# The value half of the compression two slots behind its key half, and its weights asked for behind chunk 10

## The reference

```
h = rms_norm(x)
proj = h @ w_in                  # state-space input, NSA q/k/v, gates, stick-breaking q/k/v
o_ssm = s5_mixer(...)            # diagonal complex state space
o_nsa = nsa_mixer(...)           # compressed + selected + window attention
o_sb  = stick_breaking(...)
x += (sum of gate * (branch @ w_branch)) @ w_out
x += conv_ffn(rms_norm(x))       # up, width-3 causal conv, silu * value, down
```

```
blocks = t[:, idx] + pos
hid = gelu(einsum('bnlhd,lde->bnhe', blocks, w1))    # w1: 32 x 64 x 128 floats, 1 MB
return einsum('bnhe,ed->bnhd', hid, w2)
```

## Time and profile before

| | us |
|---|---|
| median of 3 runs | 954.81 (954.48 to 955.27) |
| the profiled execution, its own time | 954.62 |
| its span | 952.9 |
| TensorE busy | 925.4 |
| VectorE busy | 709.8 |
| ScalarE busy | 592.1 |
| GpSimd busy | 287.9 |

### The profile page before, as it was taken

How to read it: one execution, slowest core, us unless ns; L and a number is a source line. 1 busy time by engine, 2 the same in 40 slices (tenths; PEclk the granted TensorE clock), 3 DMA queues, 4 the chain that set the end, 5 groups by cost and what they waited for, 6 DMA issues and landing times. The chain is left out here.

```text
span 952.9 us, 16037 instructions
## 1 busy us (share of the span) xinstructions
PE 925.4 (97%) x5855; PEld 777.3 (82%) x5855; DVE 709.8 (74%) x1131; ACT 592.1 (62%) x955; POOL 287.9 (30%) x226
## 2 busy tenths in 40 slices
PE   8889999999999999999999999999999999999996
PEld 6789877777878888888889887777787788888885
DVE  6998967666667887888875777766567677777876
ACT  7436776768455665666674567677664566666664
POOL 0523334351420568467100413443315001010110
PEclk9999999999999999999999999999999999999999
DMA  8964434453454756556449744433645456556551
GB/s 235 266 192 141 140 126 133 130 147 132 167 176 138 204 189 207 177 180 212 142 126 299 204 141 133 133 124 99 181 129 177 133 177 212 186 178 213 181 177 44
DMA packets 139559, 159.09 MB, mean 167 GB/s; under 512 B 17153, under 2 KB 106089, under 8 KB 139498
## 3 DMA queue, kind: packets, MB, share of 16 engines
q1 hardware_dynamic: 137960, 156.44, 53.2%
q10 hardware_dynamic: 1538, 1.84, 0.7%
HBM read 154.33 MB, written 1.05 MB: 163 GB/s over the span
## 5 line engine op out<-in xcount | busy, mean ns | idle before, releaser
L1719 DVE TENSOR_TENSOR wl<-ring,wh 128x1024 fp32r<-128x1024 f32 (+1 forms) x276 | 361.1, 1311 | 94.6 <-ACT wh L1384 93.5
L1384 ACT ACTIVATE wh<-ring 128x1024 fp32r<-128x1024 f32 (+1 forms) x276 | 288.2, 1045 | 148.0 <-PE pj L791 114.8
L791 PE MATMUL pj<-h,wh 128*128 128x256 f32 (+1 forms) x1376 | 296.8, 339 | 12.1 <-DVE wl L1719 11.1
L791 PEld LDWEIGHTS pj<-h,wh 128*128 128x128 f32 x1376 | 230.5, 191 | 39.5 <-issue 10.5
L791 PE MATMUL pj<-wh,h 128*128 128x512 f32 (+1 forms) x832 | 259.4, 394 | 3.0 <-DVE wl L1719 1.4
L791 PE MATMUL pj<-h,wl 128*128 128x256 f32 x1024 | 188.9, 283 | 0.0
L791 PEld LDWEIGHTS pj<-wh,h 128*128 128x128 f32 x832 | 148.4, 188 | 41.8 <-issue 8.2
L791 PEld LDWEIGHTS pj<-h,wl 128*128 128x128 f32 x1024 | 157.6, 191 | 6.6
L791 PE MATMUL pj<-wl,h 128*128 128x512 f32 (+1 forms) x416 | 159.7, 384 | 0.0
L2396 POOL TENSOR_TENSOR work<-work 128x512 f32<-128x512 f32 x20 | 41.1, 2055 | 261.7 <-DVE work L2182 198.5
L791 PEld LDWEIGHTS pj<-wl,h 128*128 128x128 f32 x416 | 78.1, 188 | 16.3
(11 more groups left out here) (303 smaller groups left out, 1230.8 us busy)
## 6 DMA issues: line engine op xcount, KB each, us to landing
ring<-in_ffn_w_up SPq DMA_DIRECT2D x44, 1024.0 KB, 5.1
ring<-in_w_in SPq DMA_DIRECT2D x40, 1024.0 KB, 5.1
ring<-in_ffn_w_down SPq DMA_DIRECT2D x22, 1024.0 KB, 4.9
ring<-in_w_in SPq DMA_DIRECT2D x16, 512.0 KB, 5.3
ring<-in_w_branch SPq DMA_DIRECT2D x8, 1024.0 KB, 5.6
ring<-in_w_out SPq DMA_DIRECT2D x8, 1024.0 KB, 5.1
ring<-in_w_branch SPq DMA_DIRECT2D x8, 512.0 KB, 5.9
ring<-in_w_in SPq DMA_DIRECT2D x8, 256.0 KB, 3.9
```

The source lines that it names most:

```text
L791: return nc.tensor.matmul(o, a, b, start=start, stop=stop, skip_group_check=True)
L1384: A(dst, src, ACT.Copy).then_inc(w_hi.sem, 1)
L1719: TT(dst, src, hi.bitcast(F32), ALU.subtract).then_inc(w_lo.sem, 1)
```

## The change

The table of slots gives the two halves slots of their own: hidden 0 and 2, output 2 and 4, with each sum one slot behind its hidden part. The functions of TensorE and ScalarE are cut accordingly, and the copies of `kc` and `vc` are put at the two output slots. SP asks for the value's weights behind chunk 10.

```diff
-CMP_HID, CMP_OUT, CMP_S, CMP_T = 0, 2, 3, 6
+CMP_HID, CMP_OUT, CMP_S, CMP_T = (0, 2), (2, 4), 3, 6
...
# SP
-                    if i == 6:
+                    if i == 10:
                         sp.wait_ge(h_turned.sem, h_turned.at(l, 4))
                         sp.sem_inc(passed.sem, 1)
                         load_cmp(l, 1)
...
# TensorE: cmp_out() loops no longer over r, but takes it
-                def cmp_out():
+                def cmp_out(r):
...
-                    if q == CMP_HID:
-                        for r in range(2):
-                            cmp_hidden(r)
-                    if q == CMP_HID + 1:
-                        for r in range(2):
-                            cmp_sum(r)
-                    if q == CMP_OUT:
-                        cmp_out()
+                    if q in CMP_HID:
+                        cmp_hidden(CMP_HID.index(q))
+                    if q - 1 in CMP_HID:
+                        cmp_sum(CMP_HID.index(q - 1))
+                    if q in CMP_OUT:
+                        cmp_out(CMP_OUT.index(q))
...
# ScalarE
-                    if q == CMP_HID:
-                        for r in range(2):
-                            a.wait_ge(hq_done.sem, hq_done.at(l, r + 1))
-                            A(hp[:, r, :], (bA, bB)[r][:, 0:P], ACT.Copy).then_inc(hq_out.sem, hq_out.up())
+                    if q in CMP_HID:
+                        r = CMP_HID.index(q)
+                        a.wait_ge(hq_done.sem, hq_done.at(l, r + 1))
+                        A(hp[:, r, :], (bA, bB)[r][:, 0:P], ACT.Copy).then_inc(hq_out.sem, hq_out.up())
...
-                    if q == CMP_OUT:
+                    if q == CMP_OUT[0]:
                         a.wait_ge(kc_done.sem, kc_done.at(l, 1))
                         A(kc[:, 0:NC], bO[:, 0:NC], ACT.Copy).then_inc(kc_ready.sem, kc_ready.up())
+                    if q == CMP_OUT[1]:
                         a.wait_ge(kc_done.sem, kc_done.at(l, 2))
                         for r in range(0, P, 32):
                             ins = A(vc[r:r + NC, r // 32, :], bB[r:r + NC, 64:64 + HD], ACT.Copy)
```

More of the change, by code:

```diff
@@ L1005, in cmp_sum @@
                         .then_inc(hid_done.sem, hid_done.up())
-                def cmp_out():
-                    for r in range(2):
[L1010 to L1020, removed]
+                def cmp_out(r):
+                    pe.wait_ge(hid_ready.sem, hid_ready.at(l, r + 1))
+                    for s in range(2):
+                        hs = hid[:, r, NC * s:NC * s + NC]
+                        if r == 0:
+                            ins = mm(bO[HD * s:HD * s + HD, 0:NC], w2[:, 0, :], hs, True, True)
+                        else:
+                            for t in range(NT):
+                                row = 32 * (2 * s + t)
+                                ins = nc.tensor.matmul(bB[row:row + NC, 64:64 + HD], hs, w2[:, 1, :], start=True,
+                                                       stop=True, skip_group_check=True, tile_position=(0, row))
+                    ins.then_inc(kc_done.sem, kc_done.up())
                 def cmp_scores():
@@ L1580, in _ @@
                         branch_hi(slice(2 * n, 2 * n + 2), oS[:, 2 * n:2 * n + 2, :])
-                    if q == CMP_HID:
-                        for r in range(2):
-                            a.wait_ge(hq_done.sem, hq_done.at(l, r + 1))
-                            A(hp[:, r, :], (bA, bB)[r][:, 0:P], ACT.Copy).then_inc(hq_out.sem, hq_out.up())
[L1585 to L1590, removed]
-                    if q == CMP_OUT:
+                    if q in CMP_HID:
+                        r = CMP_HID.index(q)
+                        a.wait_ge(hq_done.sem, hq_done.at(l, r + 1))
+                        A(hp[:, r, :], (bA, bB)[r][:, 0:P], ACT.Copy).then_inc(hq_out.sem, hq_out.up())
+                    if q - 1 in CMP_HID:
+                        r = CMP_HID.index(q - 1)
+                        a.wait_ge(hid_done.sem, hid_done.at(l, r + 1))
+                        A(hid[:, r, 0:2 * NC].rearrange("p (g n) -> p g n", g=2),
+                          (bA, bB)[r][:, P:P + 32].rearrange("p (g n) -> p g n", g=2)[:, :, 0:NC], ACT.Gelu_apprx_tanh)\
+                            .then_inc(hid_ready.sem, hid_ready.up())
+                    if q == CMP_OUT[0]:
                         a.wait_ge(kc_done.sem, kc_done.at(l, 1))
                         A(kc[:, 0:NC], bO[:, 0:NC], ACT.Copy).then_inc(kc_ready.sem, kc_ready.up())
+                    if q == CMP_OUT[1]:
                         a.wait_ge(kc_done.sem, kc_done.at(l, 2))
```

## The result

The changed kernel takes 957.97 us (median of 6 runs, 957.40 to 959.59) against 955.00 of the kernel before (6 runs, 954.48 to 955.93): a ratio of 1.0034 [1.0023, 1.0044], slower by 3.0 us. The forecast was 955.7, and the range ended at 957.4. The profiled execution took 958.56 us with a span of 956.8, against 954.62 and 952.9: 3.9 us more of span, which the two traces let us divide.

The account below looks back on a forecast made before the run. The kernel was taken as a TensorE stream with short holes. First layer 0 plus second layer's slot 6 +0.98, net of the load's 0.71 gain, gave +1.0 us: forecast 955.7, range 953.3 to 957.4.

Parts of the forecast that it names:

- The step that failed: First layer, piece 14: GpSimd's rotation product may slip ahead, TensorE starting 1.0 us later; taken as 0.
- The bound: First layer, piece 14: the slip of GpSimd's product was bounded by -0.5 and +0.4 us.
- sign of being wrong: Wrong if second layer's slot 6 hole is missing, TensorE waits again by slot 8, or pre-slot-0 holes change over 1 us.
- the stretch at 1.2 GHz: First layer: short slow stretch after TensorE's waits; VectorE sets the pace there, so it costs nothing.
- Slot 6 of the second layer: Value copies delay the exponential, VectorE's split and TensorE: slot 6 +0.98 us, with a new 1.6 us hole.
- The load's gain of 0.71 us: Second layer, before slot 0: chunk 7 comes sooner, VectorE's part of piece 15 starts 0.71 us earlier; bounds 0 and 1.5.
- The first layer's slot 6: Exponential could start at 92.20, against 92.18 before; the 0.61 us hole stays: 0, bounds -0.6 and +0.4.
- The value load: Behind chunk 10 its issues fit SP's queue; TensorE needs the weights over 15 us later: no wait, 0.
- A: Rival, slot 4: table load ahead of the copies, exponential and slot 6 1.28 us earlier; sum -0.3, 954.5; 15%.
- C: Rival, second layer: ScalarE's lateness of 3.94 us lasts, TensorE waits again at slot 8, paying 3.0: 957.8; 14%.
- D: Rival, both layers: the exponential doesn't follow its table load at once, standing 0.65 us behind: 957.0; 4%.
- B: Rival, faster: transfers were the root of more than one TensorE hole in both layers: 952.5; 12%.

Follow-up runs that it names:

- e2: Kernel before with only the value-weight load moved behind chunk 10, slots unchanged: 956.67 us, ratio 1.0011 to the kernel before.
- e5: Changed kernel with 20 unused matmuls on TensorE ahead of the first layer's piece 14: 957.54 us, ratio 1.0016 to the kernel before.
- e8: The changed kernel itself timed again, as control of a later group on one chip: 957.23 us, ratio 1.0020 to the kernel before.
- e4: Changed kernel with slot 4's exponential ahead of the value copies, softmax's small operands in their own tile: 955.90 us, ratio 1.0006 to the kernel before.
- e9: Changed kernel with the exponential ahead of the value copies and the load behind chunk 6 in both layers: 955.21 us, ratio 0.9998.
- e1: Changed kernel with the value-weight load back at its old place behind chunk 6: 956.74 us, ratio 1.0018 to the kernel before.
- e10: Changed kernel, exponential first, load moved only in the second layer, idle matmuls before the first layer's pieces 10, 11 and 14: 954.09 us, ratio 0.9989.

## Why the prediction was wrong

- **The step that failed** is the first layer's: "If such a product slips ahead of piece 14, TensorE starts the piece 1.0 us later and has 0.69 us in its next hole to get it back [...] Bounds -0.5 and +0.4, I take 0." The slip happened (e2: 57.13 in place of 59.78), and the start was late by 1.1 us, as bounded. The price was not: 1.64 us in this execution, and by time 1.5 (medians) or 1.1 (ratio) in e2, even with the second layer's gain in it. The prediction's own sign of being wrong, a hole before slot 0 that changes by over 1 us, is the 1.49 that became 2.58. The prediction had dismissed the stretch at 1.2 GHz as costing nothing. That was right for where it lay, over pieces that end in a hole; over piece 14, with TensorE itself behind, it costs 1.45 us. e5 and e8 have the slip without that clock, and lose 0.07 and 0.13 in their profiles. That this part is the clock's is shown by profiles alone; by time e5 gained nothing that could be seen.
- **The bound** was made from the hole alone, as if a longer wait had no other consequence. The trace of the kernel before had the pattern: the slow stretch that the prediction dismissed came behind two holes of 2.00 and 2.05 us (before 41.71 and 46.87) with 3.1 us of work between them. With a term of 0 to +1.6 the range would have held the result.
- **Slot 6 of the second layer** was right in mechanism and size. Without the gain ahead of it the working gives 0.98 + 0.71 = 1.69 for the stretch from the hidden matmuls; it measured 1.77. The hole was put at 1.6 and is 1.41, because TensorE's own stream grew by 0.3 us and not by the 0.1 allowed for the moved matmuls. e4, which changes only this order in the changed kernel, takes it away, and so does e9 against e1.
- **The load's gain of 0.71 us** is there in part. The wait for chunk 7 is gone, and the splits of pieces 14 and 15 stand back to back (528.94) as worked out. But ScalarE's four issues at 518.09 took 3.00 us where the profile before had 2.49, which put the next piece 0.5 us late. It isn't the load's doing: e1, with the load at its old place, shows 3.51, and the profile before was a favourable one. Kernels with the old load need 50.59 (before) and 50.90 us (e1, e9) for the stretch, those with the moved one 50.35 to 50.72 in eight profiles and 49.84 in e10, where the four issues took 2.44 us as in the profile before. Against that one like case the gain is 0.75; where both had slower issues it is 0.2 to 0.55.
- **The first layer's slot 6** came as worked out: exponential at 94.61, 22.9 us behind the hidden matmuls where it was 22.8, and the hole 0.47 in place of 0.61.
- **The value load** is in nobody's way at its new place. It landed in 7.0 us (median), and in the second layer its matmuls came 15.3 us behind the issue (531.86 and 547.19). Right.
- **Rivals.** A is refuted: the load stands behind the copies (557.91). C is refuted: after slot 6 nothing is lost (394.3 against 394.4). D is refuted: load and exponential follow the copies at 0.01 and 0.02 us. The Trainium skill's page "ScalarE: Activation LUTs" ("What ACT_TABLE_LOAD costs") has a drain of some 1380 ns besides; these rows leave no room for one. (Two such drains are an estimated 2.8 us by the page's figure, not the 2.7 of the prediction.) B, that transfers were the root of more than one hole, is refuted: the rows did come sooner, and TensorE's hole before piece 14 grew by 1.1 us, since VectorE, which the earlier trace rows shows full, sets the pace there.

What stays open: what decides in which execution the earlier slow stretch lies over piece 10 or 11, and with it whether the next can meet piece 14, and how often each happens. The starts of the profiles differ by up to 1.8 us at piece 7, but no run fixed that start. Open too is why GpSimd's product and VectorE's operation slow each other; the runs show only the price.

## What to carry to other kernels

Where the pacing engine is full and is slowed by what another engine runs beside it, an earlier transfer can be a loss: ask beside which operation the other engine's work will now run, and whether that operation stands ahead of the one that the critical engine waits for. A hole in TensorE's stream can cost twice, by its length and by the clock behind it, and in these profiles a slow stretch was free only where a hole followed; give such a term its own bound. And in an in-order queue put the copy that nobody waits for behind the operation that heads a chain, table load included: here that order is worth 1.9 us (e9 against e1), and with the first layer's load left where it was the change becomes a gain of 1.1.

## What the runs showed that had not been expected

- A single 128x512 product of GpSimd costs what VectorE does beside it 1.0 to 1.1 us in every place read, whatever that is (eight small operations, one large, a pair of splits), and GpSimd's own takes 1.3 to 2.4.
- Two executions of the same instructions differ in where TensorE is at 1.2 GHz, and one placement costs 1.5 us more than the other (18.81 and 17.30 in after and e8).
- Four 64 KB DMA issues on ScalarE's queue took from 2.44 to 3.51 us, and the engine's next instruction waits for them.
- Start-up alone moved piece 7 from 30.49 to 32.26 us over the profiles, more than most edits here are worth; stretches between two marks of the same profile are the thing to compare.
